# MLP and gated units of a two-block fp32r kernel: both operand halves in one 512-column product, with fillers in TensorE's pauses and later mixing turns

## The chip, the cores and the metric

The kernel runs on one core of one Trainium2 chip. The metric is the device time of one execution in microseconds, as the median of several runs. All arithmetic that matters is in fp32, with the large products done in three fp32r matmuls (below).

## The reference

Sequence 256, width 1024, batch 1. A first block has two layers (windowed and neighbourhood attention, then a bidirectional Mamba-2 mixer), each followed by a squared-ReLU MLP; a second block has two layers of SwiGLU, a mixer (31-tap convolution beside differential attention) and SwiGLU again. What the change touches:

```python
def squared_relu_mlp(x, w1, w2):                 # w1 1024x4096, w2 4096x1024, 2 times
    return jnp.square(jax.nn.relu(x @ w1)) @ w2
def swiglu(h, w_gate, w_up, w_down):             # 1024x2816, 1024x2816, 2816x1024, 4 times
    return (jax.nn.silu(h @ w_gate) * (h @ w_up)) @ w_down
# mixer of the second block, per layer: diff_attention over 4 heads of 2 maps
        p = jax.nn.softmax(s, axis=-1)
        a = p[:, :, 0] - lam * p[:, :, 1]
        return jnp.einsum("bhqk,bhkd->bhqd", a.astype(v.dtype), v)
# beside it, conv_module: silu(rms_norm(conv31(a * sigmoid(g))))
```

## The kernel before, in words

**Units.** All weights pass through a ring of three slots in units of 128 x 2048 fp32 values (1 MB). SyncE loads a unit into `w_raw` once VectorE has finished with the unit three before. ScalarE casts it to fp32r (`w_hi`, `split`, L744); VectorE, or GpSimd for some units of the mixers, subtracts the cast from the raw value (`w_lo`, L1134 or L646). TensorE takes a unit when `lo_ready` says so, and its last matmul counts up `unit_done`.

**Three terms.** Each product x @ w is done as hi x hi + lo x hi + hi x lo in `three` (L1694), one weight load (LDWEIGHTS) and one matmul for each. The activations stand as `op_hi` and `op_lo`, 16 chunks of 128 x 256. `project` makes a unit of 256 output columns from 8 steps of k for each of two chunks c: 48 matmuls of 256 columns into one PSUM bank `pg[:, b, :]`. `output` multiplies two new chunks of hidden values with a unit of the second matrix: 24 matmuls of 512 columns that accumulate in the four banks `acc`.

**The order in an MLP** (16 hidden groups). TensorE: projection 0, projection 1, output 0, projection 2, output 1, and so on, in a hardware loop of three groups. The projections rotate over banks 0 to 2 of `pg`. ScalarE applies ReLU from PSUM into `act_buf` (`hidden`, L797), VectorE squares it into `h32` (L1262, `h32_ready`), ScalarE casts it to `op_hi` (L804), VectorE makes `op_lo` (L1258, `h_ready`). Splits stand in between on both engines. **In a gated unit** (11 groups) a group is gate projection (bank 0), up projection (bank 1) and the output of the group before. ScalarE applies Silu to the gate (`act_done`), VectorE multiplies it by the up bank (L1265).

**Between stages** VectorE adds `acc` into X and makes norms, TensorE waits for `norm_ready` and transposes X into `pg` (`turn`, L1758 and L1759), ScalarE and VectorE evacuate it to `op_hi` and `op_lo`. The first projection of a stage starts with the first bank that is ready. `clear_sums` zeroes `acc` by four bf16 matmuls with zeros (L1834). `bias_strips` (L2080) are four matmuls for the relative bias, two at a time, inside the first gated unit.

**The mixing turns.** For each layer of the second block TensorE runs turns s = 0 to 11. Turn s < 8 has the scores of map s (L2116, L2118) and four of the 31 tap matmuls of one convolution channel group (L2135). From s = 4 each even turn transposes a mixed map (L2126), which waits for VectorE's `mix_ready`; from s = 5 each odd turn has the product with V (`o2`, L1871). Turn 10 has `csum` (L2144), turn 11 the spread of the convolution's norm (L2150). VectorE in turn s takes the scores (L1609), finds the maximum, and in odd turns from 3 mixes the two maps of a head (L1641, L1645). ScalarE exponentiates and copies the transposed maps.

## Time and profile before

| | us |
|---|---|
| median of 3 runs | 1870.94 (1869.0 to 1875.68) |
| the profiled execution, own time | 1870.63 |
| its span, first to last instruction | 1868.7 |
| TensorE matmul busy | 1798.0 (96%) |
| VectorE busy | 1071.7 (57%) |
| ScalarE busy | 864.0 (46%) |
| GpSimd busy | 285.8 (15%) |

The mean granted TensorE clock was 0.984 of full speed. Matmuls are pipelined: a record of 0.28 or 0.39 us overlaps the next, so what a matmul costs in a stream is the distance from one start to the next, or a stretch divided by its count. The chain of waits follows the work that ended last back from the end; idle time of an engine off that chain costs nothing.

### The profile page before, as it was taken

The page shows a single profiled execution, that of the slowest core. Times are in us where ns is not written, and L with a number is a line of the kernel's source. Part 1 is how long each engine was busy: PE and PEld are TensorE (multiplying, and loading weights), DVE is VectorE, ACT ScalarE, POOL GpSimd, SP SyncE. Part 2 cuts the span into 40 slices and gives each one's busy share as a digit, 9 for nine tenths or more (in the row PEclk, how much of TensorE's full clock was granted, in tenths as well). Part 3 has the DMA queues.
Part 4 walks back from the last instruction along what each step waited for, and adds up shares of the span by engine and source line. Part 5 has one row for each costly group of instructions (what it writes and reads, how often), then busy time and mean ns, then how long its engine had stood idle before and what let it go on. Part 6 is the DMA issues. An engine that isn't in the chain of part 4 may idle for free.

```text
span 1868.7 us, 29784 instructions
## 1 busy us (share of the span) xinstructions
PE 1798.0 (96%) x12211; PEld 1651.5 (88%) x12217; DVE 1071.7 (57%) x1438; ACT 864.0 (46%) x1137; POOL 285.8 (15%) x155
## 2 busy tenths in 40 slices
PE   8989999899999999989999989999999999989999
PEld 8757999899997899979998968999899989779998
DVE  5566655778576665564444674445544545745444
...
GB/s 300 113 10 150 217 187 182 156 185 149 174 1 101 165 234 187 182 134 182 185 194 135 177 72 90 186 192 185 137 203 196 184 158 167 105 45 203 183 186 103
DMA packets 211135, 293.99 MB, mean 157 GB/s; under 512 B 6426, under 2 KB 184064, under 8 KB 211056
## 3 DMA queue, kind: packets, MB, share of 16 engines
...
HBM read 291.81 MB, written 1.05 MB: 157 GB/s over the span
## 4 chain that ended last, share of the span: by engine, by line
PE 88%; DVE 7%; ACT 3%; issue 1%; DMA 0%; POOL 0%; SPq 0%; ACTq 0%; DVEq 0%
PE pg L1694 53%; PE acc L1694 26%; PE acc L2039 1%; DVE acc L1568 1%; PE pg L2135 1%; PE pg L1759 1%; PE pg L2023 1%; PE pg L2025 1%; DVE stats L1188 1%; DVE X L1185 1%; DVE arena L1629 1%; PE pg L1758 1%; ACT w_hi L744 1%; PE acc L1960 0%; PE pg L2028 0%
## 5 line engine op out<-in xcount | busy, mean ns | idle before, releaser
L1134 DVE TENSOR_TENSOR w_lo<-w_raw,w_hi 128x2048 fp32r<-128x2048 f32 x231 | 539.4, 2337 | 389.5 <-ACT w_hi L744 389.4
L1694 PE MATMUL pg<-op_hi,w_hi 128*128 128x256 f32 x2544 | 725.9, 285 | 5.0 <-DVE op_lo L1152 3.3
L1694 PE MATMUL pg<-op_lo,w_hi 128*128 128x256 f32 x2544 | 720.6, 283 | 0.0
L1694 PE MATMUL pg<-op_hi,w_lo 128*128 128x256 f32 x2544 | 720.5, 283 | 0.0
L744 ACT CAST w_hi<-w_raw 128x2048 fp32r<-128x2048 f32 x270 | 514.4, 1905 | 216.4 <-PE pg L1694 141.3
L1694 PEld LDWEIGHTS pg<-op_hi,w_hi 128*128 128x128 f32 x2544 | 488.7, 192 | 13.3 <-issue 7.1
L1694 PEld LDWEIGHTS pg<-op_hi,w_lo 128*128 128x128 f32 x2544 | 488.9, 192 | 3.3 <-issue 0.5
L1694 PEld LDWEIGHTS pg<-op_lo,w_hi 128*128 128x128 f32 x2544 | 488.7, 192 | 0.0
L1694 PE MATMUL acc<-w_hi,op_hi 128*128 128x512 f32 x768 | 302.1, 393 | 1.2 <-DVE op_lo L1402 0.9
L1694 PE MATMUL acc<-w_lo,op_hi 128*128 128x512 f32 x768 | 300.8, 392 | 0.0
L1694 PE MATMUL acc<-w_hi,op_lo 128*128 128x512 f32 x768 | 299.8, 390 | 0.0
L646 POOL TENSOR_TENSOR w_lo<-w_raw,w_hi 128x2048 fp32r<-128x2048 f32 x39 | 179.7, 4611 | 575.0 <-DVE w_lo L1134 435.9
L1694 PEld LDWEIGHTS acc<-w_hi,op_hi 128*128 128x128 f32 x768 | 145.4, 189 | 30.4 <-DVE op_lo L1402 1.4
L1694 PEld LDWEIGHTS acc<-w_hi,op_lo 128*128 128x128 f32 x768 | 145.0, 189 | 30.9
L1694 PEld LDWEIGHTS acc<-w_lo,op_hi 128*128 128x128 f32 x768 | 145.4, 189 | 27.3
L804 ACT CAST op_hi<-h 128x512 fp32r<-128x512 f32 x76 | 47.2, 621 | 251.0 <-PE acc L1694 214.1
L797 ACT ACTIVATE act_buf<-pg 128x512 f32<-128x512 f32 x76 | 45.4, 598 | 241.3 <-PE pg L1694 241.3
L1258 DVE TENSOR_TENSOR op_lo<-h,op_hi 128x512 fp32r<-128x512 f32 x76 | 57.1, 751 | 112.5 <-ACT op_hi L804 112.5
L1568 DVE SCALAR_TENSOR_TENSOR acc<-arena,pcol,acc 128x256 f32<-128x256 f32 x174 | 71.1, 481 | 0.6
L1694 PE MATMUL pg<-w_hi,op_hi 128*128 128x256 f32 (+1 forms) x240 | 68.6, 286 | 0.0
L1694 PE MATMUL pg<-w_lo,op_hi 128*128 128x256 f32 (+1 forms) x240 | 67.7, 282 | 0.0
L1694 PE MATMUL pg<-w_hi,op_lo 128*128 128x256 f32 (+1 forms) x240 | 67.7, 282 | 0.0
...
## 6 DMA issues: line engine op xcount, KB each, us to landing
...
```

Source lines behind the costliest of these rows:

```text
L646: pool.tensor_tensor(w_lo[:, r, :], w_raw[:, r, :], w_hi[:, r, :].bitcast(F32), ALU.subtract) \
L744: act.copy(w_hi[:, u % RING, :], w_raw[:, u % RING, :]).then_inc(hi_ready, 1)
L797: act.activation(act_buf[:, :], src, func).then_inc(act_done, 1)
L804: act.copy(op_hi[:, at_chunk:at_chunk + 2, :], h32[:, :].rearrange("p (c t) -> p c t", c=2)).then_inc(h_hi, 1)
L1134: dve.tensor_tensor(w_lo[:, s, :], w_raw[:, s, :], w_hi[:, s, :].bitcast(F32), ALU.subtract) \
L1185: dve.scalar_tensor_tensor(out=x, in0=x, scalar=ALPHA, in1=acc[:, q, :], op0=ALU.mult, op1=ALU.add).then_inc(x_new, 1)
L1188: ins = dve.bn_stats(stats[:, t, a, :], x)
L1258: dve.tensor_tensor(op_lo[:, dst, :], h32[:, :].rearrange("p (c t) -> p c t", c=2), op_hi[:, dst, :].bitcast(F32), ALU.subtract).then_inc( ...
L1568: ins = dve.scalar_tensor_tensor(out=conv_bank(c) if k < CK - 1 else cacc[:, c, :], in0=uu[:, c, k:k + T], scalar=w, in1=conv_bank(c), op0 ...
L1629: dve.tensor_scalar(n2[:, s, :], m2[:, s, :], -1.0, None, ALU.mult).then_inc(mx2_ready, 1)
L1694: ins = pe.matmul(psum, l, r, start=first and i == 0, stop=last and i == 2)
L1758: return pe.matmul(o, X[:, t, j * P:(j + 1) * P], diag[:, t, :], start=True, stop=True)
```

## The change

The two operand tiles become one tile `op` of 128 x 2 x 16 x 256, whose halves are `op_hi` and `op_lo`. In MLP and gated units `project_pair` replaces `project`: for each k and chunk one matmul under `w_hi` with both halves (512 columns, a whole bank: main sum left, low sum right) and one under `w_lo` with `op_hi` (256 columns, left). A projection now fills two banks. ScalarE copies the low sums to SBUF, VectorE adds the main sums to them; ReLU and square are one VectorE instruction; Silu reads SBUF. The MLP's projections all use banks 0 and 1 and wait for `h32_ready`; gate uses 0 and 1, up uses 2 and 3. The other projections (attention, Mamba, mixer) stay as they were.

`warm` issues n matmuls of bf16 zeros, 512 columns each, to a free bank: 8 before the turns `ln1_0`, `ln2_0` and `ln1_1`, 4 after `ln2_0`, 6 after the last Mamba head, 18 before the first `ffn1` turn and 4 before the second, 4 before each `mix` turn, 4 after `csum`, 8 before the transposes of the mixer's output, 4 before each `ffn2` turn. Only some of these lines are shown. In the mixing turns the transposes start at s = 6 and `o2` at s = 7, `csum` stands at s = 12 and the spread at s = 13. The bias strips move from the first gated unit to the end of the second MLP.

```diff
-        op_hi = sb("op_hi", [P, 16, T], F32R)
-        op_lo = sb("op_lo", [P, 16, T], F32R)
+        op = sb("op", [P, 2, 16, T], F32R)
+        op_hi, op_lo = op[:, 0, :, :], op[:, 1, :, :]
...
+        def main_half(b):
+            return pg[:, b:b + 2, 0:T]
+
+        def low_half(b):
+            return pg[:, b:b + 2, T:2 * T]
...
-            def hidden(h, u_in, func, src, it=None, per_h=0, per_u=0):
+            def hidden(h, u_in, it=None, per_h=0, per_u=0):
 
                 act.wait_ge(unit_done, at(u_in + 1, it, per_u))
-                act.activation(act_buf[:, :], src, func).then_inc(act_done, 1)
+                act.copy(act_pair, low_half(0)).then_inc(act_done, 1)
+
+            def gate_low(u_in, it=None, per_u=0):
+
+                act.wait_ge(unit_done, at(u_in + 1, it, per_u))
+                act.copy(act_pair, low_half(0)).then_inc(gate_lo, 1)
+
+            def gate_silu(h, it=None, per_h=0):
+
+                act.wait_ge(gate_sum, at(h - HG_FFN[0] + 1, it, per_h))
+                act.activation(act_buf[:, :], act_buf[:, :], ACT.Silu).then_inc(act_done, 1)
+
+            def up_low(h, u_in, it=None, per_h=0, per_u=0):
+
+                act.wait_ge(unit_done, at(u_in + 1, it, per_u))
+                act.wait_ge(h_ready, at(h, it, per_h))
+                act.copy(h_pair, low_half(2)).then_inc(up_lo, 1)
 
             def hidden_hi(h, u_free, it=None, per_h=0, per_u=0, at_chunk=8):
 
...
-                hidden(h0, u0, ACT.Silu, pg[:, 0, :])
+                gate_low(u0)
+                gate_silu(h0)
                 split(u0 + 3)
+                up_low(h0, u0 + 1)
                 hidden_hi(h0, None)
-                if between:
-                    between(0)
...
-                    hidden(h, u, ACT.Silu, pg[:, 0, :], it, 1, 3)
+                    gate_low(u, it, 3)
                     split(u + 3, it, 3)
+                    gate_silu(h, it, 1)
+                    up_low(h, u + 1, it, 1, 3)
...
-                    if s >= 4 and s % 2 == 0:
-                        h = DH * l + (s - 4) // 2
+                    if s >= 6 and s % 2 == 0:
+                        h = DH * l + (s - 6) // 2
                         act.wait_ge(mixT_done, h + 1)
                         if h >= 2:
                             act.wait_ge(o2_done, h - 1)
                         act.copy(pmixT[:, h % 2, :], pg[:, 2, 0:384]).then_inc(mixT_ready, 1)
-                    if s >= 6 and s % 2 == 0:
-                        o2_out(l, (s - 6) // 2)
-                    if s == 9:
+                    if s >= 8 and s % 2 == 0:
+                        o2_out(l, (s - 8) // 2)
+                    if s == 11:
 
                         act.wait_ge(cconv, l + 1)
                         act.activation(osq, cacc, ACT.Square).then_inc(csq, 1)
-                    if s == 10:
+                    if s == 12:
                         act.wait_ge(csum, l + 1)
...
-            def hidden(h, u_in, make, it=None, per_h=0, per_u=0):
+            def hidden(h, it=None, per_h=0):
                 dve.wait_ge(act_done, at(h + 1, it, per_h))
                 if h:
 
                     dve.wait_ge(h_ready, at(h, it, per_h))
-                if u_in is not None:
-                    dve.wait_ge(unit_done, at(u_in + 1, it, per_u))
-                make().then_inc(h32_ready, 1)
+                dve.tensor_tensor(h_pair, main_half(0), act_pair, ALU.add).then_inc(h_sum, 1)
+                dve.wait_ge(h_sum, at(h + 1, it, per_h))
+                dve.scalar_tensor_tensor(out=h32[:, :], in0=h32[:, :], scalar=0.0, in1=h32[:, :], op0=ALU.max,
+                                         op1=ALU.mult).then_inc(h32_ready, 1)
+
+            def gate_add(h, it=None, per_h=0):
+                dve.wait_ge(gate_lo, at(h - HG_FFN[0] + 1, it, per_h))
+                dve.tensor_tensor(act_pair, main_half(0), act_pair, ALU.add).then_inc(gate_sum, 1)
+
+            def gated(h, it=None, per_h=0):
+                dve.wait_ge(up_lo, at(h - HG_FFN[0] + 1, it, per_h))
+                dve.tensor_tensor(h_pair, main_half(2), h_pair, ALU.add).then_inc(h_sum, 1)
+                dve.wait_ge(act_done, at(h + 1, it, per_h))
+                dve.wait_ge(h_sum, at(h + 1, it, per_h))
+                dve.tensor_tensor(h32[:, :], h32[:, :], act_buf[:, :], ALU.mult).then_inc(h32_ready, 1)
 
             def hidden_lo(h, it=None, per_h=0, at_chunk=8):
                 dve.wait_ge(h_hi, at(h + 1, it, per_h))
...
                 dve.tensor_tensor(op_lo[:, dst, :], h32[:, :].rearrange("p (c t) -> p c t", c=2),
                                   op_hi[:, dst, :].bitcast(F32), ALU.subtract).then_inc(h_ready, 1)
...
             def swiglu(u0, h0):
                 split(u0 + 2)
+                gate_add(h0)
                 split(u0 + 3)
-                hidden(h0, u0 + 1, gated)
+                gated(h0)
                 hidden_lo(h0)
 
                 def group(u, h, it=None, last=False):
                     split(u + 2, it, 3)
+                    gate_add(h, it, 1)
                     split(u + 3, it, 3)
-                    hidden(h, u + 1, gated, it, 1, 3)
+                    gated(h, it, 1)
                     if last:
                         hidden_lo(h, at_chunk=10)
...
+            def project_pair(u, b, it=None, per=0, fresh=None):
+                take(u, it, per)
+                if fresh:
+
+                    pe.wait_ge(xt_ready, TURN_BANK[fresh] + 1)
+                for c in range(2):
+                    bank = pg[:, b + c, :]
+                    for k in range(KC):
+                        if fresh and c == 0 and k and k % 2 == 0:
+                            pe.wait_ge(xt_ready, TURN_BANK[fresh] + k // 2 + 1)
+                        o = k * U + c * P
+                        hi, lo = wslice(u, o, o + P)
+                        pe.matmul(bank.rearrange("p (x t) -> p x t", x=2), hi, op[:, :, k, :], start=k == 0, stop=False)
+                        ins = pe.matmul(bank[:, 0:T], lo, op_hi[:, k, :], start=False, stop=k == KC - 1)
+                ins.then_inc(unit_done, 1)
...
-            def mlp(u0, h0, fresh, between=None):
-                project(u0, pg[:, 0, :], fresh=fresh)
+            def mlp(u0, h0, fresh, between=None, late=None):
+                project_pair(u0, 0, fresh=fresh)
                 if between:
                     between()
 
                 def groups(u1, h1, it=None):
                     for j in range(3):
-                        project(u1 + 2 * j, pg[:, (1 + j) % 3, :], False, it, 6)
+                        pe.wait_ge(h32_ready, at(h1 + j, it, 3))
+                        project_pair(u1 + 2 * j, 0, it, 6)
                         pe.wait_ge(h_ready, at(h1 + j, it, 3))
                         output(u1 + 1 + 2 * j, 8, False, False, it, 6)
 
                 with pe.Fori(0, (G1 - 1) // 3 - 1) as it:
                     groups(u0 + 1, h0 + 1, it)
+                if late:
+                    late(0)
                 groups(u0 + 2 * G1 - 7, h0 + G1 - 3)
+                if late:
+                    late(2)
                 pe.wait_ge(h_ready, h0 + G1)
                 output(u0 + 2 * G1 - 1, 10, False, True)
 
-            def swiglu(u0, h0, fresh, between=None):
-                project(u0, pg[:, 0, :], fresh=fresh)
-                project(u0 + 1, pg[:, 1, :])
-                if between:
-                    between(0)
+            def swiglu(u0, h0, fresh):
+                project_pair(u0, 0, fresh=fresh)
+                project_pair(u0 + 1, 2)
 
                 def group(u, h, it=None):
 
                     pe.wait_ge(act_done, at(h, it, 1))
-                    project(u, pg[:, 0, :], False, it, 3)
+                    project_pair(u, 0, it, 3)
 
                     pe.wait_ge(h32_ready, at(h, it, 1))
-                    project(u + 1, pg[:, 1, :], False, it, 3)
+                    project_pair(u + 1, 2, it, 3)
                     pe.wait_ge(h_ready, at(h, it, 1))
                     output(u + 2, 8, False, False, it, 3)
 
                 with pe.Fori(0, G2 - 2) as it:
                     group(u0 + 2, h0 + 1, it)
-                if between:
-                    between(2)
                 group(u0 + 3 * G2 - 4, h0 + G2 - 1)
                 pe.wait_ge(h_ready, h0 + G2)
                 output(u0 + 3 * G2 - 1, 10, False, True)
+
+            def warm(bank, n):
+
+                for _ in range(n):
+                    pe.matmul(bank, zeros[:, 0:1].broadcast_to([P, P]), zeros[:, 0:1].broadcast_to([P, 512]),
+                              start=True, stop=True)
...
-            mlp(U_MLP[1], HG_MLP[1], "ln1_1", distance_bias)
+            mlp(U_MLP[1], HG_MLP[1], "ln1_1", distance_bias, bias_strips)
 
             for l in range(DEPTH):
+                warm(pg[:, 0, :], 4 if l else 18)
+                pe.wait_ge(bias_evac, DH)
                 turn(f"ffn1_{l}", None)
                 clear_sums()
-                swiglu(U_FFN[2 * l], HG_FFN[2 * l], f"ffn1_{l}", None if l else bias_strips)
+                swiglu(U_FFN[2 * l], HG_FFN[2 * l], f"ffn1_{l}")
+                warm(pg[:, 0, :], 4)
                 turn(f"mix_{l}", None)
...
-                for s in range(2 * DH + 4):
+                for s in range(2 * DH + 6):
...
-                    if s >= 4 and s % 2 == 0 and s < 2 * DH + 4:
-                        k = DH * l + (s - 4) // 2
+                    if s >= 6 and s % 2 == 0:
+                        k = DH * l + (s - 6) // 2
                         pe.wait_ge(mix_ready, k + 1)
                         if k >= 1:
                             pe.wait_ge(mixT_ready, k)
                         for o, a in ((0, 0), (P, P), (2 * P, 2 * P)):
                             ins = pe.transpose(pg[:, 2, o:o + P], pmix[:, k % 2, a:a + P], ident[:, :])
                         ins.then_inc(mixT_done, 1)
-                    if s >= 5 and s % 2 == 1:
-                        o2(l, (s - 5) // 2)
+                    if s >= 7 and s % 2 == 1:
+                        o2(l, (s - 7) // 2)
                     if s < 2 * DH:
...
-                    if s == 10:
+                    if s == 2 * DH + 4:
 
                         pe.wait_ge(cpair, l + 1)
                         pe.wait_ge(sc2_taken, 8 * l + 2 * DH)
...
                             ins = pe.matmul(pg[:, 0, t:t + 1], osq[:, 0, t * P:(t + 1) * P], ones_m, start=True,
                                             stop=True)
                         ins.then_inc(csum, 1)
-                    if s == 2 * DH + 3:
+                        warm(pg[:, 3, :], 4)
+                    if s == 2 * DH + 5:
                         pe.wait_ge(crstd, l + 1)
                         for t in range(TT):
                             ins = pe.matmul(pg[:, 1, t * P:(t + 1) * P], cdev[:, t:t + 1].broadcast_to([P, P]),
                                             ident[:, :], start=True, stop=True)
                         ins.then_inc(cspread, 1)
+                warm(pg[:, 3, :], 8)
                 pe.wait_ge(o2_evac, DH * l + DH)
```

Three places in the order of instructions. The first is TensorE at the start of an MLP, behind projection 0. Before, projection 1 (it writes the next bank) waits for its weights only:

```order
L1694 MATMUL pg<-op_lo,w_hi 128x256
L1801 UNCONDITIONAL_BRANCH
L1801 ISA
L1694 MATMUL pg<-op_hi,w_hi 128x256 [waits lo_ready]
L1694 MATMUL pg<-op_hi,w_lo 128x256
L1694 MATMUL pg<-op_lo,w_hi 128x256
L1694 MATMUL pg<-op_hi,w_hi 128x256
```

Now at the same place (`op` is the tile of both halves):

```order
L1783 MATMUL pg<-op,w_lo 128x256
L1859 UNCONDITIONAL_BRANCH
L1859 ISA
L1728 ISA [waits h32_ready]
L1782 MATMUL pg<-op,w_hi 128x512 [waits lo_ready]
L1783 MATMUL pg<-op,w_lo 128x256
L1782 MATMUL pg<-op,w_hi 128x512
```

Three matmuls of a step have become two, and a wait for the squared hidden values of group 0 stands before projection 1.

The second is VectorE at the same place: two splits, the hidden values, their low half, then the loop. Before:

```order
L1134 TENSOR_TENSOR w_lo<-w_raw,w_hi 128x2048 [waits hi_ready] x2
L1262 TENSOR_TENSOR h<-act_buf 128x512 [waits act_done]
L1258 TENSOR_TENSOR op_lo<-h,op_hi 128x512 [waits h_hi]
L1285 UNCONDITIONAL_BRANCH
L1285 ISA
L1134 TENSOR_TENSOR w_lo<-w_raw,w_hi 128x2048 [waits hi_ready]
```

Now:

```order
L1167 TENSOR_TENSOR w_lo<-w_raw,w_hi 128x2048 [waits hi_ready] x2
L1284 TENSOR_TENSOR h<-pg,act_buf 128x512 [waits act_done]
L1286 SCALAR_TENSOR_TENSOR h<-h 128x512 [waits h_sum]
L1303 TENSOR_TENSOR op<-h,op 128x512 [waits h_hi]
L1324 UNCONDITIONAL_BRANCH
L1324 ISA
L1167 TENSOR_TENSOR w_lo<-w_raw,w_hi 128x2048 [waits hi_ready]
```

One instruction, the add from PSUM, has come in between the splits and the square.

The third is TensorE in the mixing of layer 0, from the scores of turn 4 on (`arena` holds the mixer's tiles; the 128x256 rows with four instructions are taps). Before:

```order
L2116 MATMUL pg<-arena 128x128 [waits sc2_taken,qk_ready]
L2118 MATMUL pg<-arena 128x256
L2126 MATMUL pg<-ident,arena 128x128 [waits mix_ready]
L2126 MATMUL pg<-ident,arena 128x128 x2
L2135 MATMUL pg<-arena 128x256 x4
L2116 MATMUL pg<-arena 128x128 [waits sc2_taken]
L2118 MATMUL pg<-arena 128x256
L1871 MATMUL acc<-arena 128x128 [waits mixT_ready]
```

Now:

```order
L2188 MATMUL pg<-arena 128x128 [waits sc2_taken,qk_ready]
L2190 MATMUL pg<-arena 128x256
L2207 MATMUL pg<-arena 128x256 x4
L2188 MATMUL pg<-arena 128x128 [waits sc2_taken]
L2190 MATMUL pg<-arena 128x256
L2207 MATMUL pg<-arena 128x256 [waits diag_ready]
L2207 MATMUL pg<-arena 128x256 x3
L2188 MATMUL pg<-arena 128x128 [waits sc2_taken]
L2190 MATMUL pg<-arena 128x256
L2198 MATMUL pg<-ident,arena 128x128 [waits mix_ready]
L2198 MATMUL pg<-ident,arena 128x128 x2
```

The scores and taps of turns 4 and 5 and the scores of turn 6 now stand ahead of the first transposes.

## Rows read from the trace of the kernel before

**Rows 1.** The page, busy time of the engines: us, share, instructions.
```profile
PE 1798.0 (96%) x12211; PEld 1651.5 (88%) x12217; DVE 1071.7 (57%) x1438; ACT 864.0 (46%) x1137; POOL 285.8 (15%) x155
```
**Rows 2.** The page, shares of the chain that ended last, by line.
```profile
PE pg L1694 53%; PE acc L1694 26%; PE acc L2039 1%; DVE acc L1568 1%; PE pg L2135 1%; PE pg L1759 1%; PE pg L2023 1%; PE pg L2025 1%; DVE stats L1188 1%; DVE X L1185 1%; DVE arena L1629 1%; PE pg L1758 1%; ACT w_hi L744 1%; PE acc L1960 0%; PE pg L2028 0%
```
**Rows 3.** The chain in order of time: start, us, what; MLP, then gated unit.
```profile
174.85 5.47 PE acc L1694 x24
180.32 5.75 PE pg L1694 x48
...
1184.83 11.51 PE pg L1694 x96
```
**Rows 4.** Busy time by stage; columns: stretch, length, engines, clock, DMA share, GB/s.
```profile
1184.00:1329.00 145.00, 145.00 (x1035) 137.22 (x1034) 69.17 (x43) 58.65 (x44) 0.00 (x0) 1.00 0.55 186
```
**Rows 5.** TensorE in order of time, Mamba heads: start, record length, what.
```profile
561.09 0.33 PE L2028 MATMUL pg<-neg_tri,ident_r 128*128 128x256 f32 x1
561.26 0.34 PE L2023 MATMUL pg<-g_pair,select 128*128 128x384 f32 x1
```
**Rows 6.** TensorE in time, start of the Mamba projections; busy time there.
```profile
352.12 0.41 PE L1694 MATMUL pg<-op_lo,w_hi 128*128 128x256 f32 x1
352.33 0.41 PE L1694 MATMUL pg<-op_hi,w_hi 128*128 128x256 f32 x1
...
351.50:354.50 3.00, 2.97 (x14) 2.98 (x15) 2.97 (x3) 1.64 (x1) 0.00 (x0) 0.51 0.00 0
```
**Rows 7.** ScalarE and VectorE in time, start of the first MLP.
```profile
169.13 0.60 ACT L797 ACTIVATE act_buf<-pg 128x512 f32<-128x512 f32 x1 [3.35 <-PE pg L1694]
...
165.10 4.48 DVE L1134 TENSOR_TENSOR w_lo<-w_raw,w_hi 128x2048 fp32r<-128x2048 f32 x2
```
**Rows 8.** VectorE in time, gated unit, the product with a PSUM operand.
```profile
1179.40 0.69 DVE L1265 TENSOR_TENSOR h<-act_buf,pg 128x512 f32<-128x512 f32 x1 [1.05 <-PE pg L1694]
```
**Rows 9.** TensorE in time, one pair of bias strips.
```profile
834.66 1.45 PE L2080 MATMUL pg<-arena 128*128 128x384 f32 x4
```
**Rows 10.** TensorE in time, mixing turns of layer 0.
```profile
1093.25 2.00 PE L2135 MATMUL pg<-arena 128*128 128x256 f32 x8
...
1099.77 0.90 PE L2126 MATMUL pg<-ident,arena 128*128 128x128 f32 x3 [3.67 <-DVE arena L1645]
1100.46 3.62 PE L2135 MATMUL pg<-arena 128*128 128x256 f32 x8
```
**Rows 11.** Busy time by stage, mixing of layer 0; the clock is third from last.
```profile
1100.00:1110.00 10.00, 10.00 (x31) 7.42 (x31) 4.35 (x16) 2.34 (x9) 0.00 (x0) 0.56 0.00 0
```
**Rows 12.** VectorE in time, taking scores in turns 5, 6 and 7.
```profile
1105.70 0.56 DVE L1609 SCALAR_TENSOR_TENSOR arena<-pg,arena 128x384 f32<-128x384 f32 x1 [4.28 <-PE pg L2118]
...
1110.69 0.56 DVE L1609 SCALAR_TENSOR_TENSOR arena<-pg,arena 128x384 f32<-128x384 f32 x1 [1.96 <-PE pg L2118]
...
1113.75 0.56 DVE L1609 SCALAR_TENSOR_TENSOR arena<-pg,arena 128x384 f32<-128x384 f32 x1 [1.26 <-PE pg L2118]
```
**Rows 13.** TensorE in time, `csum` and spread; VectorE, the last mix.
```profile
1120.52 0.61 PE L2144 MATMUL pg<-arena 128*128 128x1 f32 x4 [1.45 <-DVE arena L1652]
1122.27 1.08 PE L2150 MATMUL pg<-ident,arena 128*128 128x128 f32 x4 [0.37 <-DVE arena L1654]
...
1117.73 0.74 DVE L1645 SCALAR_TENSOR_TENSOR arena<-arena 128x128 f32<-128x128 f32 x2
```
**Rows 14.** Waits of TensorE: us in total, times, longest.
```profile
PE pg L1758 <- DVE xn L1232: 12.5, 12, 5.3
```
**Rows 15.** TensorE in time, the turn before the second gated unit.
```profile
1151.07 2.05 PE L1758 MATMUL pg<-xn,X 128*128 128x128 f32 x16 [0.81 <-DVE xn L1232]
```
**Rows 16.** The chain in order of time, first output units behind pauses.
```profile
574.28 6.71 PE acc L1694 x24
...
1127.61 17.22 PE acc L1694 x72
...
1648.94 17.71 PE acc L1694 x72
```

40 lines of the change are left out of this document (25 added, 15 removed).

## The prediction, made before the changed kernel had run

> **What bounds the kernel now.** I read the page's busy shares first: TensorE 96%, VectorE 57%, ScalarE 46% [rows 1]. The shares of the chain that ended last agree: 53% of the span is TensorE writing `pg` at L1694 (the projections) and 26% is TensorE writing `acc` there (the output products) [rows 2]. Then I read the chain in order of time. Inside an MLP it alternates a projection of 48 matmuls in 5.75 us and an output unit of 24 matmuls in 5.47 us with nothing between; inside a gated unit two projections take 11.51 us [rows 3]. The table by stage says the same of a whole loop: TensorE busy 145.00 of 145.00 us, VectorE 69.17, ScalarE 58.65 [rows 4]. So in the loops only TensorE's own matmuls count, and VectorE has some 76 us free in each such stretch. Outside the loops TensorE waits for norms and for the attention steps.
>
> **Term 1, the paired product.** A unit's projection has 2 column chunks times 8 steps of k. Before, each step is three matmuls of 256 columns, each with its own weight load; now it is one of 512 columns (main and low halves of the operand under `w_hi`) and one of 256 (`w_lo`). The columns stay 768 per step; one matmul and one weight load go. From [rows 3], 5.75/48 = 0.1198 us for a matmul of 256 columns and 5.47/24 = 0.228 us for one of 512. New unit: 16 x 0.228 + 16 x 0.1198 = 5.57 us, against 5.75. That is 0.187 us saved (with unrounded 5.755 and 5.475). Units changed: 16 in each of two MLPs and 22 in each of four gated units, 120 in all. 120 x 0.187 = 22.4 us off the path, because the loops leave no idle time.
> Both ends of this cost: if the 512-column matmul carried no gap over its columns (512/2.4 GHz = 0.213, and 0.107 for 256), the unit would be 5.12 us and the term 76 us; that needs every gap to vanish although 0.228 still shows one with the longest cover. At the other end stands the new access pattern, two pieces of 256 columns from tiles 16 KB apart. The nearest row with its operand in two pieces is L2028 (256 columns): the next matmul starts 0.17 us after it [rows 5], 0.05 more than 0.12. The matmul behind it waits for a semaphore, so this is a ceiling: 16 x 0.05 = 0.8 us a unit, +74 us after the 22 saved. I take the middle value, since the 512-column rows are the same size and run in the same stream.
> The Trainium skill ("TensorE: Matmul & The Clock Gate", section "Back-to-back issue gap") gives N/2.4 + 2.5 ns between warm matmuls. By that rule 16 matmuls fewer save 16 x 2.5 = 40 ns a unit, 4.8 us in all. By that rule the total would be 1856.
>
> Against that rule the rows show 13 to 15 ns over the columns instead of 2.5, so the trace disagrees. At the low clock (granted 0.51 over 351.5 to 354.5, nearly all of it at 1.2 GHz) the spacing is 0.21 us [rows 6], 256/1.2, with no gap at all, so a unit in a slow stretch gains nothing.
>
> **Term 2, the sum on VectorE.** ScalarE now copies the low half out of PSUM (as large as the old activation, 0.60 us [rows 7]); VectorE adds the main half and then squares, or adds twice and multiplies. A 512-column add with a PSUM operand takes 0.69 us [rows 8]. Per MLP group VectorE gets 0.69 us more, per gated group 1.38 us, ScalarE 0.6 and 1.2 us. VectorE's free half covers it. Who waits: the next projection now uses the same bank pair, so it waits for `h32_ready` instead of having a third bank. The chain is 0.60 + 0.69 + 0.69 and three hops (0.02 to 0.05 each between engines), about 2.1 us; in the loop the output unit (5.47 us) covers it. Were the cover gone, it would be 2.1 us for each of 32 groups. It is gone once per MLP, at the start, where projection 1 followed projection 0 directly. Projection 0 is evacuated from 169.13 on, and VectorE is in two weight splits until 169.58 [rows 7], so the square ends near 171.2 against 169.1: +2.1 us. In the second MLP the distance-bias matmul lies between and hides 0.7: +1.4. Together +3.5 us. In a gated unit gate and up have their own pairs; the gate pair is needed again only after up's 5.57 us, so its copy, add, Silu and one split fit: 0. At the tails the longer chain (copy, add, multiply, hi, lo, 3.3 us and hops, about 3.9) ends within the 5.47 us of the last but one output: 0.
>
> **Term 3, bias strips.** Four matmuls of 384 columns are exposed twice in the first gated unit, 1.28 us each time (their records span 1.45) [rows 9]. They move into the second MLP, also between full-rate matmuls: 2.6 off, 2.6 on, net 0.
>
> **Term 4, later mixing turns.** TensorE stands 3.67 us at L2126 until VectorE's first mix is ready, and behind it in its queue stand the scores of turns 4 to 7 [rows 10]. Then it is slow: eight tap matmuls take 3.62 us instead of 2.00 [rows 10], the granted clock over 1100 to 1110 is 0.56 [rows 11]. VectorE in turn idles 4.28, 1.96 and 1.26 us for those scores, 7.5 in all [rows 12]. With the transposes two turns later, TensorE does the scores of turns 4 and 5 in that pause. Walking the turns with the row durations: VectorE's turn 5 starts at 1101.4 instead of 1105.7, turn 7 ends near 1109.0, its next wait (for the last taps, held back in turn 7 behind the first `o2`, which needs ScalarE's copy at 1107) is about 0.7 us, and the last mix ends near 1112 against 1118.4 [rows 13]. ScalarE still has copies, `o2_out` and the square ahead of the sum, so `csum` comes near 1115.3 instead of 1120.5 [rows 13]: -5.2 us. What is late next: the four fillers stand between `csum` and the last `o2`, and push it and the column spread back by 0.85, of which about 0.5 reaches the output product. Net -4.7 a layer, two layers: -9.4 us. Bounds: 0 (another chain, ScalarE's, was as late) and -15 (all of VectorE's idle time).
>
> **Term 5, fillers.** At full clock a 512-column filler takes near 0.21 us. Where they stand TensorE waits 12.5 us at L1758 over 12 waits, 5.3 at the longest [rows 14]; the tightest place is 0.81 us [rows 15] for four fillers of 0.85: no cost. What they may give back is the slow start of the work behind pauses: output units at 6.71 instead of 5.47 (1.24), 17.22 and 17.71 instead of 16.4 for 72 matmuls (0.8, 1.3) [rows 16], and 16 matmuls at 0.21 instead of 0.12 at the start of the SSM projections (1.5) [rows 6]. Sum 4.8; the fillers are short against pauses of 5 to 13 us, so I take 3.5. Bounds: 0 and 4.8; a cost of up to 0.9 for each of five tight places if the fillers themselves run slow.
>
> **Sum.** -22.4 + 3.5 + 0 - 9.4 - 3.5 = -31.8 us. The profiled execution took 1870.6 us (span 1868.7), 0.3 below the median of the runs, 1870.94. 1870.6 - 31.8 = 1839.
>
> **Rivals.** (a) Time goes by columns: a paired matmul with its operand from two tiles takes twice a single one, 0.24 us. The unit stays at 16 x 0.24 + 16 x 0.12 = 5.75 and the pair term at 0: +3.5 - 9.4 - 3.5 = -9.4, 1861. For it: at the low clock there is no gap to save. Against: the 0.228 of the 512-column rows. 0.10.
> (b) The pairs pay but nothing else does: the mixing is held by ScalarE's order, the fillers run out before the pause ends. -22.4 + 3.5 = -18.9, 1852. For it: `csum` depends on ScalarE's square, not on VectorE alone. Against: 7.5 us of VectorE idle before it. 0.13.
> (c) The MLP turnaround slips past its cover: two splits (4.48 us [rows 7]) queued ahead of the add and its 2.1 us make 6.6, 1.1 more than the output unit covers; in every sixth of 32 groups that is +6, 1845. For it: splits and hidden values share both queues in order. Against: VectorE is free half the time. 0.07.
> (d) The 256-column matmul was held by its weight load, which now hides under 512 columns; all gaps go. -76 in place of -22.4: 1785. Against: the gap of 0.228 rows. 0.05.
> (e) Slower: the paired matmul pays for its two pieces. With the other terms at -9.4 it decides from 16x + 1.92 = 5.755 + 9.4/120, x = 0.245 us; at the 0.278 us of the ceiling in term 1 the pair term is +74, the total near 1935. For it: only [rows 5], read as if nothing waited. Against: both records of L2028 fit a wait behind them. 0.04.
>
> **How the numbers follow.** Forecast 1839 with 0.61; rivals as given. About 0.3%, 5.6 us, is what a measurement here can tell from no change (the three runs lie within 0.36%). The forecast's own range is 1829 to 1848; stretched to (b), (c) and most of (a) it is 1820 to 1860, with (d), (e) and some of the tails out. Faster 0.93 (all but (e) and the upper tail of (a)), same 0.03, slower 0.04.
>
> **What would show it.** Right: projections of 32 matmuls in 5.5 to 5.6 us, back to back with outputs of 5.47; a single pause near 2 us before the second projection of each MLP; no VectorE wait over 1 us for scores in turns 5 to 7; output product of the mixing beginning some 5 us earlier after its last projection. Wrong: a projection of 5.7 or more, starts of 512-column matmuls over 0.245 us apart, waits for `h32_ready` inside the loops, or fillers at whose end the norm was already ready.

## The result, and the profile after

The changed kernel takes 1854.5 us (median of 5 runs, 1851.5 to 1858.2); the kernel before, run beside it, 1870.1 us. The ratio is 0.991 (95% interval 0.989 to 0.993). So it is faster, inside the range of 1820 to 1860, but by about half of what was forecast: 15.6 us and not 31.8. The profiled execution took 1856.8 us (span 1855.0).

TensorE is as busy in us as before [rows 1], with 1831 matmuls fewer; VectorE and ScalarE have more. First the engines' line of the page, then the busy time of the stretch of [rows 4]: VectorE went from 69.17 to 82.85 us in it, and TensorE still has no idle time.
```profile
PE 1797.3 (97%) x10380; PEld 1546.9 (83%) x10393; DVE 1151.9 (62%) x1558; ACT 910.8 (49%) x1225; POOL 285.5 (15%) x155
```
```profile
1184.00:1329.00 145.00, 145.00 (x762) 123.51 (x761) 82.85 (x62) 66.74 (x62) 0.00 (x0) 1.00 0.56 188
```
The chain in order of time, output units only, first of the first MLP, then of the gated unit of [rows 3]:
```profile
192.92 5.46 PE acc L1735 x24
204.03 5.46 PE acc L1735 x24
...
1191.27 5.50 PE acc L1735 x24
1208.06 5.50 PE acc L1735 x24
```
From one output unit to the next an MLP group takes 11.11 us (before 11.22) and a gated group 16.79 (before 16.98, [rows 3]: 11.51 + 5.47). The forecast had 11.03 and 16.61. TensorE in order of time in a projection, with start and record length (records overlap, so the distance of starts is the price):
```profile
1173.64 0.40 PE L1782 MATMUL pg<-op,w_hi 128*128 128x512 f32 x1
1173.88 0.28 PE L1783 MATMUL pg<-op,w_lo 128*128 128x256 f32 x1
1174.00 0.40 PE L1782 MATMUL pg<-op,w_hi 128*128 128x512 f32 x1
1174.23 0.28 PE L1783 MATMUL pg<-op,w_lo 128*128 128x256 f32 x1
```
The mean distance is 0.2355 us from a 512-column product to the 256-column one behind it, and 0.1171 us from there to the next: 0.3526 a step, where the rows of before gave 0.228 + 0.120 = 0.348.

The two starts of an MLP's second projection, the waits that term 2 spoke of:
```profile
174.41 0.75 PE L1782 MATMUL pg<-op,w_hi 128*128 128x512 f32 x1 [2.21 <-DVE h L1286]
...
640.12 0.49 PE L1782 MATMUL pg<-op,w_hi 128*128 128x512 f32 x1 [1.47 <-DVE h L1286]
```
The mixing of layer 0, TensorE, against [rows 10, 13, 16]: the pause of 3.67 us is gone, one of 2.40 stands further back and is ended by ScalarE; `csum` is 4.9 us earlier, but 8.1 us lie between it and the output product, by the starts of their records. Before it was 6.7, from 1120.52 [rows 13] to this record (the piece of the chain in [rows 16] begins later, at 1127.61, because the record before it in the chain is still running):
```profile
1127.26 0.78 PE L1694 MATMUL acc<-w_hi,op_hi 128*128 128x512 f32 x1
```
After:
```profile
1104.71 0.59 PE L2190 MATMUL pg<-arena 64*128 64x256 f32 x2
1107.71 0.49 PE L1935 MATMUL acc<-arena 128*128 128x128 f32 x2 [2.40 <-ACT arena L1120]
...
1115.60 0.61 PE L2216 MATMUL pg<-arena 128*128 128x1 f32 x4 [1.67 <-DVE arena L1693]
1116.29 1.22 PE L1892 MATMUL pg<-zeros 128*128 128x512 bf16 x3
...
1119.43 2.18 PE L1892 MATMUL pg<-zeros 128*128 128x512 bf16 x8
1121.95 1.17 PE L2236 MATMUL pg<-ident,arena 128*128 128x128 f32 x8 [0.34 <-DVE arena L1704]
1123.71 0.50 PE L1735 MATMUL acc<-w_hi,op 128*128 128x512 f32 x1 [0.60 <-DVE op L1708]
```
Stages, from the first projection of one to that of the next, in the profiled executions (us). "Two by two" and "best" are experiments below.

| stage | before | after | pairs alone | two by two | best |
|---|---|---|---|---|---|
| up to first MLP | 161.96 | 165.13 | 161.20 | 165.38 | 165.52 |
| MLP 0 | 187.35 | 189.56 | 188.12 | 188.23 | 184.18 |
| Mamba | 278.87 | 276.21 | 278.42 | 276.79 | 276.79 |
| MLP 1 | 194.77 | 198.06 | 196.94 | 197.14 | 197.12 |
| gated 0 | 196.17 | 190.74 | 190.43 | 188.58 | 188.58 |
| mixing 0 | 136.86 | 131.80 | 135.86 | 131.48 | 130.11 |
| gated 1 | 192.84 | 190.78 | 190.41 | 188.63 | 188.67 |
| gated 2 | 192.85 | 190.79 | 190.43 | 188.65 | 188.64 |
| mixing 1 | 136.14 | 133.40 | 134.35 | 131.89 | 132.30 |
| gated 3 and end | 190.92 | 188.49 | 188.50 | 186.72 | 186.72 |

Each column is one execution. The first stage lies between 161 and 168 us in all fourteen kernels of this study, with no relation to what differs in their code: its 3.2 us between before and after is not explained here. The mixing stages vary likewise, by 2.5 to 4.6 us where the code is the same.

### The profile page after: what moved, and what is told of

It is laid out like the page before. It is cut to its first block, busy times and chain, and to the rows that moved or that the text cites. A ratio compares the mean times of both kernels' runs of the same rounds, so it can differ in the third digit from the quotient of the medians.

```text
span 1855.0 us, 26461 instructions
## 1 busy us (share of the span) xinstructions
PE 1797.3 (97%) x10380; PEld 1546.9 (83%) x10393; DVE 1151.9 (62%) x1558; ACT 910.8 (49%) x1225; POOL 285.5 (15%) x155
## 4 chain that ended last, share of the span: by engine, by line
PE 87%; DVE 8%; ACT 4%; issue 1%; DMA 0%; POOL 0%; SPq 0%; ACTq 0%; DVEq 0%
PE acc L1735 26%; PE pg L1782 24%; PE pg L1735 16%; PE pg L1783 12%; PE acc L2106 1%; DVE acc L1609 1%; ACT w_hi L757 1%; PE pg L2090 1%; PE pg L2092 1%; PE acc L2024 1%; DVE arena L1670 1%; DVE stats L1221 1%; PE pg L1816 1%; PE pg L1815 1%; DVE X L1218 1%
## 5 line engine op out<-in xcount | busy, mean ns | idle before, releaser
L1782 PE MATMUL pg<-op,w_hi 128*128 128x512 f32 x1920 | 684.0, 400 | 6.3 <-DVE h L1286 3.7
L1783 PE MATMUL pg<-op,w_lo 128*128 128x256 f32 x1920 | 539.3, 281 | 0.0
L1735 PE MATMUL acc<-w_hi,op 128*128 128x512 f32 x1536 | 489.3, 391 | 3.9 <-issue 1.7
L1782 PEld LDWEIGHTS pg<-op,w_hi 128*128 128x128 f32 x1920 | 361.6, 188 | 99.5 <-issue 8.2
L1783 PEld LDWEIGHTS pg<-op,w_lo 128*128 128x128 f32 x1920 | 363.4, 189 | 2.7
L1735 PEld LDWEIGHTS acc<-w_hi,op 128*128 128x128 f32 x1536 | 288.3, 188 | 67.6 <-issue 2.0
L1735 PE MATMUL acc<-w_lo,op 128*128 128x512 f32 x768 | 299.4, 390 | 0.0
L1735 PE MATMUL pg<-op,w_hi 128*128 128x256 f32 x1248 | 231.0, 285 | 3.0 <-DVE op L1193 1.2
L1735 PEld LDWEIGHTS pg<-op,w_hi 128*128 128x128 f32 x1248 | 196.2, 192 | 5.2 <-issue 4.1
L1735 PE MATMUL pg<-op,w_lo 128*128 128x256 f32 x624 | 176.5, 283 | 0.0
L1735 PEld LDWEIGHTS acc<-w_lo,op 128*128 128x128 f32 x768 | 144.3, 188 | 27.9
L1735 PEld LDWEIGHTS pg<-op,w_lo 128*128 128x128 f32 x624 | 119.6, 192 | 0.6 <-issue 0.5
L1735 PE MATMUL pg<-w_hi,op 128*128 128x256 f32 (+1 forms) x480 | 88.4, 284 | 0.0
```

What stands on the lines that cost most here:

```text
L1735: ins = pe.matmul(psum, l, r, start=first and i == 0, stop=last and i == 2)
L1782: pe.matmul(bank.rearrange("p (x t) -> p x t", x=2), hi, op[:, :, k, :], start=k == 0, stop=False)
L1783: ins = pe.matmul(bank[:, 0:T], lo, op_hi[:, k, :], start=False, stop=k == KC - 1)
```

## The experiments

Each was timed beside the kernel before, whose median was 1870.1 to 1871.4 us and whose low-clock time was 63 to 67 us. The 95% interval of a ratio is 0.0013 to 0.0022 to either side, 2.5 to 4 us, so a difference of that size between two medians is not shown by the medians alone. Low-clock time is the time at the lower of TensorE's two levels, 1.2 GHz, worked out from the mean granted clock c of each run of time t as 2(1 - c)t, and averaged over the runs.

| kernel | us (range) | ratio to before | low-clock us |
|---|---|---|---|
| before | 1870.1 | 1 | 64 |
| after | 1854.5 (1851.5 to 1858.2) | 0.991 | 33 |
| operand halves side by side | 1856.2 (1850.8 to 1860.6) | 0.991 | 33 |
| pairs alone | 1858.2 (1856.5 to 1863.4) | 0.993 | 63 |
| no fillers | 1858.1 (1852.5 to 1862.5) | 0.992 | 64 |
| free pair at MLP 0's start | 1851.2 (1850.4 to 1852.2) | 0.989 | 30 |
| sweeps | 1849.7 (1849.2 to 1859.8) | 0.989 | 38 |
| old turns | 1859.0 (1855.6 to 1861.9) | 0.994 | 31 |
| turns alone | 1862.4 (1860.9 to 1875.1) | 0.996 | 57 |
| free pair, no filler behind csum | 1848.8 (1846.9 to 1856.6) | 0.988 | 33 |
| these two and sweeps | 1842.7 (1842.6 to 1848.3) | 0.986 | 30 |
| two by two | 1843.4 (1839.4 to 1845.3) | 0.985 | 29 |
| free pair, no filler behind csum, two by two | 1838.5 (1835.3 to 1844.3) | 0.982 | 32 |
| one block behind | 1852.6 (1849.3 to 1854.4) | 0.989 | 34 |

### Does the operand in two pieces cost?
```
-        op = sb("op", [P, 2, 16, T], F32R)
+        op = sb("op", [P, 16, 2, T], F32R)
```
The halves of a k block lie side by side, so the 512 columns are one piece.

> The changed kernel, but the operand tile is laid out 128 x 16 x 2 x 256, so that the paired matmul reads 512 neighbouring columns and writes a bank as one piece. In the changed kernel a paired matmul is followed by the next after 0.236 us, against 0.228 for the plain 512-column matmuls. Theory A (the two pieces, 16 KB apart, cost the difference): the distance falls to 0.228, a projection unit from 5.64 to about 5.52 us, and 120 units give 13 us: 1841 to 1846 us. Rival B (the pieces cost nothing, a 512-column matmul between 256-column ones takes 0.236 for another reason): distance 0.236, unit 5.64, time as the changed kernel's, 1852 to 1857 us.

Measured: distances 0.2358 and 0.1169 us, the same as after, and 1856.2 us. The two pieces cost nothing.

### Parts: the pairs alone, and without fillers
Pairs alone is the changed kernel with the old mixing turns and no fillers; the other keeps the later turns and drops the fillers only:
```
             def warm(bank, n):
-                for _ in range(n):
+                for _ in range(0):
```


> The changed kernel without any filler and with the mixing turns of the kernel before; what is left is the paired product, its sums and the moved bias strips. Theory: the pair term is 120 x 0.112 = -13.4 us (from 5.755 to 5.643 us a unit), the waits before projection 1 of the two MLPs +3.7, slow-clock time behind the wait up to +1.7: 1860 to 1862 us from 1870. Rival (the pair term is larger, and fillers or turns cost time): under 1856. Rival (the gain came from turns and fillers alone): over 1866.

> The changed kernel without any of its fillers. Theory C (fillers keep the clock up behind pauses): the slow starts of the Mamba projections (1.5 us) and of the output products after the mixers and heads (1 us each) return, +3 to +5 us, 1857 to 1860. Rival D (the slow stretches are as frequent with fillers, they only move): 1853 to 1856, and the mean granted clock stays near 0.99.

Measured: the pairs alone give 12.4 us, more than the theory's 8 to 10 and less than the first rival's, with the same distances (0.2351, 0.1169). Without fillers the changed kernel is 3.7 us slower by the medians, with ranges that overlap, and its low-clock time goes from 33 us back to 64, that of before. Pairs alone and no fillers differ in the turns only, and their medians are equal (1858.2 and 1858.1): without fillers the later turns give nothing on top of the pairs. The slow time is seen at the mixing of layer 1. The busy time from 1619.5 to 1643.5 us, without fillers and then with them (third from last is the granted clock), and behind these TensorE's first output products without fillers, 0.57 us apart:
```profile
1619.50:1643.50 24.00, 19.89 (x69) 16.44 (x70) 10.19 (x26) 13.92 (x40) 0.00 (x0) 0.52 0.00 0
```
```profile
1619.50:1643.50 24.00, 18.68 (x87) 14.18 (x89) 11.84 (x32) 15.17 (x45) 0.00 (x0) 0.86 0.00 1
```
```profile
1638.36 0.77 PE L1735 MATMUL acc<-w_hi,op 128*128 128x512 f32 x1
1638.93 0.63 PE L1735 MATMUL acc<-w_lo,op 128*128 128x512 f32 x1
```
Without fillers TensorE works at half clock through almost the whole stretch, and that stage takes 136.71 us; with them 133.40. Not all of this is the fillers' work. 1.6 us of it lie between the stage's first projection and `csum`, where neither kernel has a filler, and the kernels of the sweeps and of the missing filler below, which have the fillers ahead of the output, are as late at `csum` there (99.4 us into the stage). The output part behind it is what the fillers ahead of it change: 29.7 us without them, 27.8 with them.

### The wait at the start of the first MLP
```
-                        project_pair(u1 + 2 * j, 0, it, 6)
+                        if it is not None or h1 != HG_MLP[0] + 1 or j:
+                            pe.wait_ge(h32_ready, at(h1 + j, it, 3))
+                        project_pair(u1 + 2 * j, 2 if h1 < HG_MLP[1] else 0, it, 6)
```
From its second projection on the first MLP writes `pg` 2 and 3, which are free at that second projection, so it waits for no evacuation. ScalarE and VectorE read those banks for these groups (not shown), and the first pass of the MLP loop is written out ahead of it.

> The changed kernel, but in the first MLP only projection 0 uses banks 0 and 1 of pg, and all later ones use banks 2 and 3, so that projection 1 needs no wait for the squared values of group 0 (the first three groups stand ahead of the loop on TensorE). Theory E (the wait of 2.2 us also lets the clock fall, five steps behind it run at half speed): -2.2 and -1.7, 1850 us. Rival F (the slow stretch behind it is chance or comes from the norm's pause): -2.2 alone, 1852, and slow matmuls still show within the first 15 us of that MLP. The second MLP keeps its wait of 1.5 us either way.

Measured: 1851.2 us. The stage takes 185.63 us against 189.56 after; two other kernels that keep the wait show 188.11 and 188.33. So the wait costs some 2.5 us (2.21 in its row), and the rest, 1.4 us, is a slow stretch that followed the wait in the profiled execution of after (the granted clock is 0.51 from 174.4 to 177.8), which comes in some executions only. With the free pair the clock is 1.00 from 161 to 176. The median lies between the theory's 1850 and the rival's 1852, so it doesn't tell whether the wait brings the slow stretch.

### Whole sweeps of one size
```
                         pe.matmul(bank.rearrange("p (x t) -> p x t", x=2), hi, op[:, :, k, :], start=k == 0, stop=False)
+                    for k in range(KC):
+                        o = k * U + c * P
+                        hi, lo = wslice(u, o, o + P)
                         ins = pe.matmul(bank[:, 0:T], lo, op_hi[:, k, :], start=False, stop=k == KC - 1)
```


> The changed kernel, but within a chunk all eight 512-column matmuls (under w_hi) come first and then all eight of 256 columns (under w_lo), in place of taking turns. In the changed kernel a pair takes 0.2355 + 0.1171 = 0.3526 us, where the rows of before give 0.228 + 0.120 = 0.348. Theory G (each change between the two sizes costs): inside the sweeps the distances are 0.228 and 0.120, a unit 5.57 to 5.60 us in place of 5.64, 120 units save 5 to 9 us: 1846 to 1850. Rival H (a 512-column matmul that reads the operand and loads weights from the weight ring takes 0.2355 whatever stands beside it): 0.2355 and 0.117 to 0.120 again, 1852 to 1858.

Measured: output units in the chain of waits, MLP and gated:
```profile
194.73 5.47 PE acc L1735 x24
205.76 5.47 PE acc L1735 x24
...
1195.03 5.47 PE acc L1735 x24
1211.64 5.47 PE acc L1735 x24
```
Groups come every 11.03 and 16.61 us: a projection of 11.03 - 5.47 = 5.56 us, the forecast's own 5.57. So its price holds for products among their own size, and the loss is in the order. The median fell by 4.8 us only (four of the five runs lie at 1849.2 to 1849.8), though the shorter groups are worth 32 x 0.08 + 44 x 0.18 = 10.5. Part of the rest is at the first projection of each stage, whose operand comes out of the norm piece by piece. The waits there (us in total, times, longest), of the sweeps and then of after:
```profile
PE pg L1782 <- DVE op L1185: 3.6, 7, 0.9
```
```profile
PE pg L1782 <- DVE op L1185: 2.3, 4, 0.9
```
In a sweep TensorE has no 256-column product to do while it waits for a piece, and all eight are left at the end: the first 32 products of gated 1 take 6.56 us where after they take 5.89. MLP 1 took 200.5 us, against 198.1 after, though its groups are shorter. 0.7 us of that is its first projection, and 1.6 us a stretch at low clock behind the wait for `h`, which the profile of after doesn't have there (the sweeps first):
```profile
641.60:645.00 3.40, 3.40 (x9) 2.70 (x10) 2.67 (x11) 3.11 (x4) 0.00 (x0) 0.56 0.90 305
```
```profile
640.10:643.50 3.40, 3.38 (x19) 3.01 (x20) 2.66 (x11) 3.11 (x4) 0.00 (x0) 1.00 1.05 369
```
The profiled execution of the sweeps was the slowest of its five (1859.8), but the combined kernel below, whose profile is of its fastest (1842.6), has a slow stretch there too (MLP 1 199.6 us). What brings it isn't shown.

### The later turns, taken back and alone
The old turns in the changed kernel, and the new turns in the kernel before, are the same edit in the two directions, in ScalarE's and TensorE's loops over the turns (here one of its places):
```
-                    if s >= 4 and s % 2 == 0 and s < 2 * DH + 4:
-                        k = DH * l + (s - 4) // 2
+                    if s >= 6 and s % 2 == 0:
+                        k = DH * l + (s - 6) // 2
```


> The changed kernel with the mixing turns of the kernel before (transposes from turn 4), fillers and pairs kept. Theory I (the later turns save what VectorE waited for): the mixer's output begins 3 to 5 us later in each layer, +6 to +9 us, 1860 to 1863. Rival J (ScalarE's copies, which now come behind all eight exponentials, give most of it back): +0 to +4, 1853 to 1858.

> The kernel before with the later mixing turns alone (no pair, no filler). Theory I: 1861 to 1865 from 1870.7, with VectorE's waits for scores in turns 5 to 7 (7.5 us in the kernel before) gone. Rival J: 1867 to 1870, VectorE's waits gone, but TensorE waits instead for ScalarE's copy of the first transposed map and the column sum comes less than 2 us earlier.

Measured: alone they give 8.2 us (1862.4), mixing stages of 132.43 and 132.76 instead of 136.86 and 136.14. In the changed kernel taking them back costs 4.6 us by the medians, less than the 6 to 9 of the theory; in the profile 4.6 us of it are in layer 0 (136.42 for 131.80) and 0.3 in layer 1 (133.69 for 133.40). And without fillers, above, they gave nothing. The chain of the turns alone shows `csum` to output product at 7.2 us (1119.43 to 1126.66; 7.0 by the starts of the records), and the output beginning slowly:
```profile
1119.43 0.60 PE pg L2144 x4
1120.04 0.57 PE acc L1871 x2
...
1124.72 1.94 PE pg L2162 x8
1126.66 13.39 PE acc L1694 x51
```
Why one comparison gives 8.2 us, one 4.6 and one nothing is seen when all profiles are put side by side. Each kernel has two mixing stages; the columns are means in us, from the first projection to `csum`, from there to the first output product, and from there to the next stage:

| turns and fillers | stages | to `csum` (range) | to output | rest | sum |
|---|---|---|---|---|---|
| old, none | 4 | 99.8 (98.8 to 101.4) | 7.0 | 29.0 | 135.8 |
| old, with fillers | 2 | 100.2 (98.8 to 101.5) | 7.1 | 27.8 | 135.1 |
| later, none | 4 | 97.2 (95.9 to 99.4) | 7.1 | 29.4 | 133.7 |
| later, with fillers | 12 | 97.4 (95.9 to 99.4) | 8.3 | 27.8 | 133.5 |
| later, none behind `csum` | 6 | 97.1 (95.9 to 99.4) | 6.7 | 27.8 | 131.6 |

With the later turns `csum` stands at 95.9 to 96.1 us when the stretch ahead of it had no low-clock time (nine stages), at 97.4 to 97.7 when it had 3.4 us (eight), and at 98.0 to 99.4 when it had 8.4 to 12 us (five). With the old turns it stands at 98.8 with 3.4 us and at 99.4 to 101.5 with 7 to 10. So the later turns bring `csum` 1.2 us forward at 3.4 us of low clock, some 2 to 3 us at 10, and 2.7 on the mean of the stages; what the clock does in one execution is as large. The six stages with old turns all have low-clock time ahead of `csum`, so a part of that may be the turns' own doing; six stages don't settle it.

### The filler behind `csum`
```
                     if s == 2 * DH + 4:
                         ...
-                        warm(pg[:, 3, :], 4)
```
on top of the free pair above.

> The kernel with the free pair in the first MLP (1851.2 us) without the four fillers behind csum. Theory K (they stand in the chain to the last o2, 0.85 us each layer, 0.5 of it on the path): the time from csum to the first output matmul falls from 8.1 to about 7.5 us, -1 us in all, 1850. Rival L (the clock falls in that place without them): the output product starts at half speed, +1 to +2 us a layer, 1853 or more.

Measured: 1848.8, 2.4 us less than with the filler; the ranges overlap (1846.9 to 1856.6 against 1850.4 to 1852.2), so the traces decide. TensorE at the same place as after (above): `csum` to output 6.5 us instead of 8.1.
```profile
1115.88 0.61 PE L2220 MATMUL pg<-arena 128*128 128x1 f32 x4 [1.67 <-DVE arena L1693]
1116.35 0.47 PE L1939 MATMUL acc<-arena 128*128 128x128 f32 x2
...
1121.23 1.11 PE L2239 MATMUL pg<-ident,arena 128*128 128x128 f32 x8
1122.40 0.50 PE L1735 MATMUL acc<-w_hi,op 128*128 128x512 f32 x1
```
Four fillers had come to a free engine, but `o2` and the spread stood behind them: 1.6 us in layer 0, where 0.5 was forecast. It is so in the other profiles too: without the filler `csum` to output takes 6.4 to 7.4 us in six stages, with it 7.8 to 9.0 in twelve (table above). In layer 1 of this profile the whole stage took 134.6 us, longer than with the filler, because `csum` came late (99.4 us), ahead of the place of the filler.

### Which part of the order costs
Two kernels. The first joins the free pair, the missing filler and the sweeps. The second is the changed kernel with products two by two (512, 512, 256, 256):
```
-                        ins = pe.matmul(bank[:, 0:T], lo, op_hi[:, k, :], start=False, stop=k == KC - 1)
+                        if k % 2 == 0:
+                            continue
+                        for m in (k - 1, k):
+                            o = m * U + c * P
+                            hi, lo = wslice(u, o, o + P)
+                            ins = pe.matmul(bank[:, 0:T], lo, op_hi[:, m, :], start=False, stop=m == KC - 1)
```


> Three cuts in one kernel: the first MLP's second projection goes to the free banks (pg 2 and 3), the mixing stages have no filler behind csum, and each output chunk of a paired projection does its eight 512-column products first and its eight 256-column ones after them. Theory L (the three act in different places and add up): from 1848.8 us (the kernel with the first two) another 120 x (5.643 - 5.57) = 8.8 us go, so about 1840, ratio to the kernel before 0.983 to 0.985; MLP groups every 11.03 us, gated groups every 16.61. Rival M (with no pauses left between sizes the chip's activity rule or the softer low-clock time takes part of it back): 1844 to 1848, the distances being those of L and the low-clock time above 45 us. Rival N (order of sizes was worth only what one run showed): 1848 or more.

> The changed kernel with the order of a chunk's products changed from 512, 256, 512, 256 to 512, 512, 256, 256: half as many changes between the two sizes, everything else as it was. Theory G (each change between sizes costs the same): half of the 0.07 us a projection that the full sweep gave, so 5.605 us a projection, MLP groups every 11.07 us (11.107 with single alternation, 11.027 with sweeps), gated groups every 16.70, the time about 120 x 0.037 = 4.4 us below the changed kernel, near 1850. Rival O (what costs is that the 256-column product adds into the same bank as the product just before it, not the change of size): then the 512 and 256 products that meet on a bank are what matters, in sweeps they meet on it just the same, and the period stays at 11.107 or goes by something other than the count of changes.

Measured: the first 1842.7, where the sum of the parts was 1840. The second 1843.4 alone, 11 us below the changed kernel (its shorter groups are worth 32 x 0.094 + 44 x 0.206 = 12.1) and more than 6 us below what its theory gave. Its output units in the chain, and a piece of a projection:
```profile
1186.91 5.45 PE acc L1735 x24
1203.49 5.45 PE acc L1735 x24
1208.95 0.45 PE pg L1782 x2
1209.40 0.23 PE pg L1788 x2
1209.63 0.47 PE pg L1782 x2
1210.10 0.23 PE pg L1788 x2
1210.33 0.46 PE pg L1782 x2
```
Four products take 0.70 us (1209.63 to 1210.33), groups 11.01 and 16.58. By the count of changes of size (16 a projection where whole sweeps have 4 and after 32) it should have been 11.07 and 16.70. So the theory under which I had read the sweeps, a fixed cost for every change, fell: changes cost nothing that shows when each size comes at least twice. The rival in that run (an addition into the bank just written) fell too: two by two and in the sweeps every product still adds into the bank just written, and the loss is gone.

### Alone, or of the same block?
The first kernel joins two by two, the free pair and the missing filler. The second is the changed kernel in an order that is shown here against two by two: it puts each 256-column product one block later (512(0), 512(1), 256(0), 512(2), 256(1), ..., 512(7), 256(6), 256(7)), so that it no longer reads what the product ahead of it has read:
```
-                        if k % 2 == 0:
+                        if k == 0:
                             continue
-                        for m in (k - 1, k):
+                        for m in (k - 1, k) if k == KC - 1 else (k - 1,):
```


> The order 512, 512, 256, 256 together with the first MLP's second projection in the free banks (pg 2 and 3) and no filler behind csum. From the kernel with that order alone (1843.4 us): the free banks save what they saved before (about 3.3 us by the medians 1854.5 and 1851.2), the filler behind csum another 2.4: about 1838, range 1835 to 1841, ratio 0.982 to 0.984. Against the same with whole sweeps (1842.7) the twos should win some 4 to 5 us: 0.016 us of each group's period, and the first projection of each stage, which in a sweep reaches its last normalised pair before it has done any 256-column product. If it comes out above 1842, the parts don't add up and the order of the sizes is not what made 1843.4.

> The changed kernel with each 256-column product put one block later: 512(0), 512(1), 256(0), 512(2), 256(1), ... 512(7), 256(6), 256(7). Sizes alternate nearly as often as in the changed kernel (12 or more changes in 16 products), but no 256-column product reads or adds where the 512-column product just ahead of it has read (another block's columns of op_hi). Theory P (a lone 256-column product costs more because it follows the 512-column product of its own block, whose columns it reads again): the loss goes, 5.57 us a projection, MLP groups every 11.02 us, gated groups every 16.60, the time 1843 to 1846. Theory Q (a 256-column product alone between two of 512 columns costs, whatever it reads; in pairs or more of one size it doesn't): 5.63 us a projection, 11.10 and 16.77, the time 1852 to 1855.

Measured: the best takes 1838.5 us (ratio 0.982, 0.980 to 0.984), as expected, 16 us below the changed kernel. One block behind takes 1852.6; its groups come every 11.08 and 16.72 us. That is near "alone" (11.10 and 16.77) and far from the other theory (11.02 and 16.60): 6 of a chunk's 8 small products stand alone there. From the two ends (8 of 8 alone: 11.107 and 16.793; none: 11.013 and 16.587) 6 of 8 gives 11.083 and 16.742. So a 256-column product alone between two of 512 costs some 6 ns, whatever it reads ((16.793 - 16.587)/32 in a gated group). In every order here that leaves a 256-column product alone a 512-column one stands alone too, so the 6 ns may as well belong to that one or to the pair. Why isn't settled either: no run here separates a product's weight load from its columns.

## Why the prediction was right, and where its size was off

The direction and the mechanism held: fewer, wider matmuls in the loops, VectorE's free half takes the sums, and TensorE never waits in the loops for it. The sum missed by 16 us. By the medians the pairs with their waits (terms 1 to 3) gave 12.4 of 18.9 us, and turns and fillers on top of them (terms 4 and 5) 3.7 of 12.9.

- **Term 1, forecast -22.4, measured -11.8.** This is the first of two terms that were mis-sized: "New unit: 16 x 0.228 + 16 x 0.1198 = 5.57 us". The two prices came from rows in which each size has its own size for neighbours, and the new stream sets every 256-column product alone between two of 512. There the step takes 0.3526 us, and the output unit behind a gated pair 5.50 us instead of 5.47. By the periods: 32 MLP groups x 0.113 + 44 gated groups x 0.187 = 11.8 us. The same work two by two gives 32 x 0.207 + 44 x 0.393 = 23.9 us, so the forecast's prices were right for another order of the same instructions. Rival (a), two pieces, was shown false by the operand halves side by side. Rivals (d) and (e) didn't occur: no gap vanished, and the mean distance stayed at 0.2355, below 0.245. The row of L2028 behind (e) was no measure of two pieces of operand: that product reads 128 columns twice.
- **The rule weighed in term 1.** The Trainium skill's N/2.4 + 2.5 ns ("TensorE: Matmul & The Clock Gate", section "Back-to-back issue gap") would have given -4.8 us for the term. The trace disagrees: the 11.8 us measured lie between the rule and the rows, and the two-by-two order at the rows.
- **Term 2, forecast +3.5, measured +3.7** (2.21 and 1.47 us), and one slow stretch behind the first of them. Rival (c) didn't occur: the waits after show two for `h` at L1286, both at MLP starts.
- **Term 3, forecast 0, held:** the two groups of strips take 1.29 us each in their new place (the chain has them at 773.58 and 808.10), and the first gated unit is 5.4 us shorter, of which 2.1 is pairs and 2.6 strips.
```profile
773.58 1.29 PE pg L2149 x4
```
- **Term 4, forecast -9.4, measured some -3 to -4.** This is the second mis-sized term, though the mechanism is as forecast: VectorE no longer waits for scores in turns 5 to 7, and in layer 0 of this profile `csum` is 4.9 us earlier (5.2 forecast). The two mixing stages are 7.8 us shorter than before (5.05 and 2.75), but that is one execution against another, with term 5's share in it. On the mean of all stages (table above) the later turns shorten a mixing stage by 1.6 us with fillers and 2.1 without. By the medians they are worth 8.2 us in the kernel before, 4.6 in the changed one and nothing beside the pairs without fillers. Three sizes were off. `csum` comes 2.7 us earlier on the mean instead of 5.2. The fillers behind `csum` push the output back by 1.6 us a layer on the mean instead of 0.5. And in layer 1 the six tap matmuls behind the new pause still take 2.77 us instead of 1.46, so the pause keeps part of its cost in slow clock:
```profile
1621.22 0.49 PE L1935 MATMUL acc<-arena 128*128 128x128 f32 x2 [2.56 <-ACT arena L1120]
...
1622.22 2.77 PE L2207 MATMUL pg<-arena,xn 128*128 128x256 f32 x6
```
- **Term 5, forecast -3.5, measured between nothing and -3.7** by the medians: with the later turns the fillers give 3.7 us (1858.1 to 1854.5), with the old turns none (pairs alone 1858.2, old turns 1859.0). By stages, the Mamba stage takes 276.2 to 277.1 us in the ten kernels with fillers and 278.0 to 279.0 in the four without, some 2 us; in the mixing the output part is 1.2 to 1.6 us shorter, which the fillers behind `csum` give back; and MLP 1 loses 1.1 to 1.6, where 18 fillers stand ahead of the first gated unit (198.1 to 198.5 for 196.9).
- **Rival (b)** (1852, only the pairs pay) lies 2.5 us below the measured 1854.5. It was right that turns and fillers pay little (3.7 us of 12.9) and wrong on the pairs, which alone reach 1858.2 and not 1852.

The time fell inside the stretched range, 1820 to 1860, but outside the forecast's own of 1829 to 1848.

The parts don't add up exactly. Pairs alone give 12.4 us, though their loops less the waits make 11.8 - 3.7 = 8.1. In the profiles, 10.1 of the 14.1 us by which pairs alone is shorter than before lie in the MLP and gated stages, and the other 4 in stages whose code it leaves as it was (2.8 in the mixing). The time of the pieces at low clock differs from execution to execution and is as large as what is left (the slowest and the fastest run of one kernel differ by 2 to 14 us), and that part stays open.
